# A hybrid decoder layer on one Trainium2 core: index scores in pieces of at most 512 columns placed between input-projection products, the sample tile alternating with tile 7, and the sample's index steps between chunks of u and q

## What is computed

```python
h = rms_norm(x, ln1)
u, q, k, v, qi, ki, wi, gates = split(h @ w_in)
# index scores: for every query and causal key, over 4 index heads
score[t, s] = sum_h w[t, h] * relu(qi[t, h] . ki[s])
idx = top_k(score, 256)                  # ties: lower position first
out = softmax_attention(q, k[idx], v[idx], bias)
pool = causal windows 2/4/8/16 over u, minus u, then a linear map
x = x + merge(pool, out, sigmoid(gates)) @ w_out ; then the FFN
```

## Time and profile before

| what | us |
|---|---|
| median of 3 runs | 1776.0 (1774.52 to 1786.52) |
| profiled execution, device time | 1784.01 |
| its span, first to last instruction | 1782.2 |
| PE busy in the span | 1672.0 (94%) |
| DVE / ACT / POOL busy | 775.4 / 478.9 / 447.4 |

### The profile page before, as it was taken

One profiled execution on the slowest core, in us unless ns is written; L12 is line 12 of the kernel. 1 busy time (PEld: TensorE's weight loads), 2 busy tenths in 40 slices (PEclk: granted clock), 3 DMA queues, 4 the chain that ended last, 5 costly groups with the idle time before them and its releaser, 6 DMA issues.

```text
span 1782.2 us, 25675 instructions
## 1 busy us (share of the span) xinstructions
PE 1672.0 (94%) x10060; PEld 1425.0 (80%) x10060; DVE 775.4 (44%) x1927; ACT 478.9 (27%) x923; POOL 447.4 (25%) x379
## 2 busy tenths in 40 slices
PE   7997799688999998899999999999999999999997
PEld 4544366445569866688889999999999999999996
DVE  2215999997910066511244442323323323323315
ACT  2113211154452255521143322111121121111113
POOL 3000107220524432111112252232232232232220
PEclk9996899899999999999999999999999999999999
DMA  5500511072651000122301231111111111111002
GB/s 174 105 21 24 172 36 37 12 272 88 195 189 48 24 1 1 44 78 82 95 25 36 71 95 48 41 46 43 36 50 44 47 47 47 47 47 47 0 1 107
DMA packets 115842, 116.95 MB, mean 66 GB/s; under 512 B 17438, under 2 KB 104110, under 8 KB 112685
## 3 DMA queue, kind: packets, MB, share of 16 engines
q1 hardware_dynamic: 102471, 73.74, 13.8%
q0 software_dynamic: 5312, 39.33, 6.9%
q10 hardware_dynamic: 7982, 2.83, 0.6%
HBM read 107.66 MB, written 8.45 MB: 65 GB/s over the span
## 4 chain that ended last, share of the span: by engine, by line
PE 55%; DVE 1%; ACT 1%; DMA 0%; issue 0%; DVEq 0%; ACTq 0%
PE banks L108 52%; PE banks L1669 3%; DMA out_dram<-yo 0%; DVE yo L1993 0%; PE banks L1658 0%; ACT XH L1826 0%; DVE rinv L1958 0%; ACT junk L1900 0%; ACT sH L1819 0%; ACT resid L1823 0%; PE banks L1761 0%; PE banks L1707 0%; DVE gated L1913 0%; ACT fst L1902 0%; ACT rinv L1870 0%
## 5 line engine op out<-in xcount | busy, mean ns | idle before, releaser
L108 PE MATMUL banks<-hnH,wH 128*128 128x344 f32 x1056 | 338.7, 321 | 3.8 <-DVE sg L1967 3.8
L108 PE MATMUL banks<-hnH,wL 128*128 128x344 f32 x1056 | 337.4, 320 | 0.0
L1791 POOL TENSOR_TENSOR wL<-w_raw,wH 128x1024 fp32r<-128x1024 f32 (+1 forms) x55 | 155.8, 2849 | 204.2 <-ACT wH L1850 203.8
L108 PEld LDWEIGHTS banks<-hnH,wH 128*128 128x128 f32 x1056 | 198.9, 188 | 4.4 <-issue 4.3
L108 PEld LDWEIGHTS banks<-hnH,wL 128*128 128x128 f32 x1056 | 198.8, 188 | 0.0
L1981 DVE TENSOR_TENSOR resid<-resid,banks 128x344 f32<-128x344 f32 x264 | 134.9, 512 | 107.4 <-PE banks L108 107.3
L1339 DVE TENSOR_SCALAR_CACHE_REDUCE pta<-SC,thr 128x384 uint8<-128x384 f32 (+2 forms) x192 | 176.1, 942 | 4.6 <-POOL SC L835 2.5
L108 PE MATMUL banks<-aH,wH 128*128 128x344 f32 x528 | 169.4, 321 | 1.6 <-DVE resid L1981 1.6
L108 PE MATMUL banks<-aH,wL 128*128 128x344 f32 x528 | 169.7, 321 | 0.0
L108 PE MATMUL banks<-hnL_lo,wH 128*128 128x344 f32 x528 | 169.0, 320 | 0.0
L108 PE MATMUL banks<-aL,wH 128*128 128x344 f32 x528 | 168.5, 319 | 0.0
(11 more groups left out here) (295 smaller groups left out, 2924.7 us busy)
## 6 DMA issues: line engine op xcount, KB each, us to landing
w_raw<-in_w_gate_up_dram SPq DMA_DIRECT2D x44, 512.0 KB, 3.9
w_raw<-in_w_down_dram SPq DMA_DIRECT2D x11, 1024.0 KB, 4.8
big<-in_w_in_dram SPq DMA_DIRECT2D x12, 512.0 KB, 4.0
W<-in_x_prompt_dram SPq DMA_DIRECT2D x8, 512.0 KB, 6.9
slab_raw<-in_w_in_dram SPq DMA_DIRECT2D x8, 512.0 KB, 4.3
x_nat<-in_x_prompt_dram SPq DMA_DIRECT2D x8, 512.0 KB, 4.1
slab_raw<-in_w_out_dram SPq DMA_DIRECT2D x8, 512.0 KB, 4.0
out_dram<-yo SPq DMA_DIRECT2D x8, 512.0 KB, 2.6
```

The costliest lines, as they stand in the source:

```text
L108: last = nc.tensor.matmul(out, w_cols(w, k), x_cols(x, k), start=(k == 0 and j == 0), stop=(k == nk - 1 and j == 2))
L1791: gp.tensor_tensor(wL[p], w_raw[p], f32(wH[p]), ALU.subtract).then_inc(w_lo, 1)
```

## The change

It does these things:

1. The scores are cut into 40 units of at most 512 columns, on banks 2 and 3. The units of tile i stand between the products of natural tile i + 3 (tiles 2 to 4) and between the products of u chunks 0, 1, 2 (tiles 5, 6, 7). Relu and sums go by unit.
2. Natural tiles 7 and 8 are made together, their products alternating.
3. Natural transposes go to banks 0 and 1, two tiles late, in the middle of a natural.
4. u and q chunks use three banks (5 to 7); chunk 3 stands in the sample index's set-up, chunks 4 to 10 between the requests' transposes and products, 11 to 13 between the last steps, 14 to 23 behind. The loops are written out.
5. The tie sums go from in front of the cached-key steps to behind step 12 (`TIES_AT`).
6. On DVE the masks of tiles 4 and 5 go behind the sample's mask, and the sample's softmax steps from inside the last bisection to in front of it; the PE steps beside the pool projections move by one.
7. `kid`, `kidT`, relu's buffers and the scratch of x's squares lie elsewhere, so the first two gathers of index keys no longer wait for the scores.

The diff, cut to its core:

```diff
+            TIES_AT = 12
+            UNITS = [(i, h, c0, min(512, lens[i] - c0)) for i in range(FIRST_TOPK, NBLK) for h in range(IH) for c0 in range(0, lens[i], 512)]
...
+                def score_unit(n):
+                    i, h, c0, w = UNITS[n]
+                    half = slice(h % 2 * HD, h % 2 * HD + HD)
+                    pe.wait_ge(natT_evac, i + 1)
+                    if n >= 2:
+                        pe.wait_ge(relu_done, n - 1)
+                    mm(ps[:, 2 + n % 2, 0:w], qiT[half, h // 2, tile_cols(i)], kiT[half, c0:c0 + w], start=True, stop=True).then_inc(idx_ready, 1)
...
+                def natural(tiles, scored):
+                    for t in tiles:
...
+                        pe.wait_ge(hT_ready, 2 * t + 2)
+                        if t >= 2:
+                            pe.wait_ge(nat_evac, t - 1)
+                    for q in range(2 * KD):
+                        k = q % KD
+                        for t in tiles:
...
+                        if scored and q % (2 * KD // len(scored)) == 0:
+                            score_unit(scored[q * len(scored) // (2 * KD)])
+                        if q == KD - 1 and tiles[0] >= 2:
+                            transpose_natural(tiles[0] - 2)
...
+                def slab_chunk(x, scored=()):
...
+                    if x < NCH:
+                        pe.wait_ge(nat_evac, NT)
+                    else:
+                        pe.wait_ge(uq_evac, x - 2)
+                    for k in range(KD):
+                        last = mm(ps[:, 5 + x % 3, 0:CH], big[:, n % 2, k, :], hT[:, k, chunk(c)], start=k == 0, stop=k == KD - 1)
+                        if scored:
+                            score_unit(scored[k])
...
+                slab_chunk(0, units_of(5))
+                transpose_natural(NT - 2)
+                slab_chunk(1, units_of(6))
                 transpose_natural(NT - 1)
+                slab_chunk(2, units_of(7))
...
+                slab_chunk(3)
                 pe.wait_ge(zi_copied, 1)
...
+                    if b < NB - 1:
+                        slab_chunk(4 + b)
                     pe.wait_ge(kidT_evac, b + 1)
...
+                slab_chunk(11)
                 pe.wait_ge(sidx_relu, 1)
...
+                slab_chunk(12)
                 pe.wait_ge(ssp_done, 1)
...
+                    if m == TIES_AT:
+                        sum_sample_ties()
...
-                        if blocks == (6, 7) and r == 20:
-                            sample_max()
-                            sample_negmax()
-                            sample_weights()
...
-                for k, i in enumerate((2, 3, 4, 5)):
+                for k, i in enumerate((2, 3)):
...
+                for k, i in ((2, 4), (3, 5)):
+                    to_mask(k, i)
+                sample_max()
+                sample_negmax()
+                sample_weights()
                 bisect_pair(slice(5, 7), (6, 7), 5 * BITS, 4 * BITS + 2)
```

More of the change, by code:

```diff
@@ L480, in _ @@
                 transpose_x(0)
[L481 to L486, removed]
+                for t in range(NT - 1):
+                    if t >= 3:
+                        pe.wait_ge(natT_evac, t - 2)
+                    transpose_x(t + 1)
+                    if t < NT - 2:
+                        natural((t,), units_of(t - 3))
+                    else:
+                        natural((t, t + 1), units_of(t - 3))
@@ new lines, in _, with sum_sample_ties @@
+                last.then_inc(stT_ready, 1)
+                slab_chunk(13)
+                pe.wait_ge(uq_evac, 12)
+                for g in range(NG):
+                    last = tr(ps[0:POOLBUF + NB, 1, g * P:(g + 1) * P], U[:, g, 16 + SEQ - POOLBUF:16 + TOK], ident[:, :])
+                last.then_inc(uT_ready, 1)
+                for x in range(14, UQ):
+                    slab_chunk(x)
+                def sum_sample_ties():
+                    pe.wait_ge(sm_step, SM["ties"])
+                    pe.wait_ge(upto_made, 1)
+                    mm(ps[:, 6, 0:P + 2], same16[:, :, :].rearrange("p b r -> p (b r)"), seq[:, :], start=True, stop=True)
+                    mm(ps[:, 6, 256:256 + P + 1], upto16[:, :], seq[:, 0:P + 1], start=True, stop=True).then_inc(sm_made, 1)
@@ new lines, in _ @@
+                pool.wait_ge(setup_step, 8)
+                load_kid(0)
+                load_kid(1)
+                for i in range(FIRST_TOPK, NBLK - 2):
+                    causal(i)
+                pool.wait_ge(nat_evac, NT)
+                for f in range(2):
+                    gp.tensor_tensor(zw[:, f * 32:(f + 1) * 32].rearrange("b (c h) -> b c h", c=NB),
+                                     ident[0:NB, 0:NB].unsqueeze(2).to_broadcast([NB, NB, IH]),
+                                     wiN[0:NB, NBLK, :].unsqueeze(1).to_broadcast([NB, NB, IH]), ALU.mult).then_inc(zw_made, 1)
@@ L843, in _ @@
+                causal(NBLK - 2)
+                causal(NBLK - 1)
+                for b in range(2, NB):
+                    pool.wait_ge(kid_used, b - 1)
+                    load_kid(b)
                 pool.wait_ge(setup_step, 3)
@@ L863, in did @@
                     ins.then_inc(mix_step, 1)
-                pool.wait_ge(uq_evac, 6 + 12)
+                pool.wait_ge(uq_evac, 12)
                 pool.wait_ge(stT_evac, 1)
-                pool.wait_ge(sidx_used, NB)
+                pool.wait_ge(ssc_ready, 1)
+                for b in range(2):
+                    pool.wait_ge(nat_out[b], 48 * len(range(b, NT, 2)))
                 did(gp.tensor_copy(sx[:, :, :, POOLBUF], U[:, :, 16 + SEQ:16 + TOK]))
@@ L1025, in _ @@
                   ACT.Copy).then_inc(qid_ready, 1)
+                for x in range(3):
+                    for n in units_of(5 + x):
+                        relu_unit(n)
+                    uq_out(x)
                 act.wait_ge(zi_ready, 2)
```

235 lines of the change are left out of this document (102 added, 133 removed).

## The result

Measured beside each other, the changed kernel takes 1829.2 us (median) and the kernel before 1781.3 us; the ratio is 1.0252, 95% interval 1.0214 to 1.0291. The forecast was 1788 with a range of 1770 to 1808: the direction of its likeliest case was right, the size was not. On the profiled executions, of which the sum was made, the spans are 1782.2 and 1827.5 us: **+45 instead of +12**.

A forecast was written before the change was run, and what follows sets the result against it. PE bound the kernel, with DVE's selection 26 us behind; delayed 37.5 us, DVE would take over. Gates 11.7 us later plus 0.3 made +12 on the 1776 us median, or 1788, range 1770 to 1808.

The forecast's parts named there:

- likeliest case: DVE's last mask comes late and sets the gates: 11.7 us later, span +12, time 1788 us; chance 0.73.
- slack: How much later DVE's selection may end before it delays the first gate product: 26 us.
- the remainder of the chain: DVE's work from the sample scores being ready, at 266, to its last mask, at 528.2.
- The request at 7.74 us: Sample index on PE: each request takes 3.10 us plus a 4.64 us chunk that hides the wait for ACT's copy.
- PE up to the sample scores: PE's new order summed as far as `ss_ready`, which the second bisection awaits: 266 us, bounds 243 and 281.
- naturals as before, "128.4": PE's naturals end as now at 129.0, less one group of five transposes: 128.4 us.
- a possible drop of the clock: At u chunk 0 on PE, behind a 3.2 us wait, the clock may drop, costing 0.7 us.
- changes into and out of a unit: PE's stationary-shape changes around the 40 score units: 80 at 0.12 us, 9.6 us in all.
- chunk 12 behind the small products: Last u chunk before `ss_ready` on PE, behind L530 and L532, priced like other chunks at 4.64 us.
- rival 2: Clock stays low through scores and chunks 0 to 2: `ss_ready` 32 us later, time 1820; chance 0.10.
- the 45 us of idle PE before the gates: PE, 33 us ahead, reaches the end of the pool projections and waits some 45 us for DVE's mask through ACT.
- plus 0.3: Behind the gate start, PE's restart at half clock costs about what it does today, plus 0.3 us.

The follow-up runs named there:

- a_ht_first: Changed kernel with DVE copying tile t+1's transposed x before scaling tile t+2; ratio 1.0227, span 1815.4 us.
- e_kv_early: Changed kernel with ACT copying tile 7's key and value bank in mid-naturals, u chunk 0 waiting for that copy alone; ratio 1.0196, span 1814.0 us.
- f_serial: Changed kernel with the naturals of tiles 7 and 8 one after the other instead of alternating; ratio 1.0173, span 1810.1 us.
- i_three_causes: Changed kernel with DVE's transposed-x copy first, tile 7's key/value bank copied early, and naturals 7 and 8 in series; ratio 1.0102, span 1796.6 us.
- b_ss_early: Changed kernel with u chunks 4 to 12 moved behind the transpose of SP1, so the sample-index steps stand together; ratio 1.0202, span 1818.5 us.

## Why the prediction was wrong

**Right, and shown.** That DVE's chain takes over and sets the gates; its slack (26, measured 25.7); PE's wait before the ties behind step 12 (17 to 20, came 18.9); the remainder of the chain (528.2 - 266 = 262.2 us forecast, 264.4 measured); the 3.5 us from the last mask to the gates (3.65). The request at 7.74 us, with ACT's copy and the gathers hidden, came at 7.66. The alternation was forecast at 3.0 us and cost 2.8. DVE's wait before the second bisection was forecast at 20 us and came at 20.4, but by luck in part: the end of the first bisection (forecast 246, came 274.5) and `ss_ready` were late by nearly the same.

**Wrong: the term "PE up to the sample scores", 266 instead of 294.9.** Term by term:

| term of the sum | forecast, us | measured, us |
|---|---|---|
| naturals as before, "128.4" | no new wait | +12.2 (a_ht_first) |
| the wait before chunk 0 and "a possible drop of the clock" behind it | 3.2 + 0.7 | 13.2 (e_kv_early), some 11 of it clock |
| changes into and out of a unit | 0.12 each, 9.6 | 0.39 a unit, 15.6 |
| alternation with the 8-row tile | 3.0 | 2.8 (f_serial) |
| chunk 12 behind the small products | 4.6 | 6.4 |

The excesses are 12.2 + 9.3 + 6.0 - 0.2 + 1.8 = 29.1, and the total is 28.9. The 12.2 hold the 1.0 us that was there ahead of the edit, so the sum closes to about 1 us and no better.

The first line is a step that failed, not a size: the working listed the waits that the change adds at tiles 7 and 8 and at chunk 0, and passed over the new `hT_ready` in `transpose_natural`, because before the change x's preparation was never late by more than 1.4 us in PE's rows. On ACT it stood behind 9 us of output issues, hidden. Of what was measured, 3.4 us are the lower clock behind the two stalls, for which the sum had no term at all.

The second was named as rival 2, with chance 0.10 and 32 us, for a clock low through three chunks. It stayed low through one, 11 us of loss: what the rival described, a clock brought down by this wait, happened at a third of its size. Whether the 64-row products kept it down is not shown. The term of 0.7 us assumed that the clock comes back almost at once behind the wait. In the forecast's own rows the clock stood at 0.50 over 21 us with PE busy for 19.5 of them, which spoke against that.

The third had its price from two places where the shape changes for one product. Around a unit both changes count. A chunk step with its 384-column unit takes 192.16 - 190.54 = 1.62 us, of which 0.58 is the product of the chunk (4.64 / 8) and 0.645 the unit (384 at 1.68 ns); with a 512-column one 204.72 - 202.89 = 1.83, less 0.58 and 0.86: 0.39 each time.

```profile
190.54 0.85 PE L531 MATMUL banks<-hT,big 128*128 128x344 f32 x2
191.32 0.91 PE L471 MATMUL banks<-I 64*128 64x384 f32 x2
192.16 0.84 PE L531 MATMUL banks<-hT,big 128*128 128x344 f32 x2
...
202.89 0.84 PE L531 MATMUL banks<-hT,big 128*128 128x344 f32 x2
203.66 1.12 PE L471 MATMUL banks<-I 64*128 64x512 f32 x2
204.72 0.85 PE L531 MATMUL banks<-hT,big 128*128 128x344 f32 x2
```

TensorEngine Tiling (Array Packing), section Key Properties, in the Trainium skill, says that changing the tiling mode drains TensorE; the 0.39 us agree with a drain in kind, and the page gives no figure.

The last line, chunk 12: in its 6.4 us the granted clock was 0.50 from about 289 to 292.3 (some 1.7 us of loss), with no stall of PE in front of it since one of 1.11 us at 277.5.

```profile
287.51 6.59 PE L531 MATMUL banks<-hT,big 128*128 128x344 f32 x16
```

**Wrong beside that, without effect on the time:** the 45 us of idle PE before the gates. The working set PE's 33 us of gain against DVE's delay as if the wait at the ties were gone, and in the same forecast had 17 to 20 us of wait there. The two waits share what PE is ahead: 18.9 + 34.5 = 53.4 us in the changed kernel, 16.3 + 34.7 = 51.0 in i_three_causes.

**Wrong and small: "plus 0.3" behind the gate start.** It came at +2.3. The clock was at 0.50 for 2.4 us longer than before, which accounts for 1.2 us; b_ss_early has as little of it as the kernel before and still +2.1, so the rest stays open.

That the three corrections together land on 265.3 is in part luck: that kernel has no alternation and no pause at chunk 0, which the forecast's 266 included with 6.9 us, and has 7.8 us of dearer unit changes and chunk 12 in their place. What the agreement does show is the chain behind it.

**The range.** With the slack used up, each us of error in `ss_ready` is a us of the result, so the range should have been at least as wide as the bounds of that sum, and its upper bound of 281 priced the changes of shape double but held no unknown wait and no longer stretch of low clock.

## What to carry to other kernels

Before making a busy engine busier, find the other long chain and what it needs first: here 19 us of gate start were to be had by moving the tie sums and the softmax steps alone, and every us that delayed DVE's input beyond its slack was lost. When a wait is added in the middle of a stage, look up how late the awaited producer really is in the trace of before, on its own engine and on the one behind it, and not at how long the consumer waited. An idle engine in front of a late input can be filled with rounds of work whose inputs are complete.

## What the runs showed of the hardware

- A pause of 2.24 us (1.90 in a second kernel) behind 60 us or more at full clock was followed by the lower clock level for some 24 us (20), though PE was busy without a gap behind it, with 64-row products between the others; a pause of 1.34 us, or of 0.32 us, in the same place was not. Stalls of 6.64 and 2.38 us with only 128-row products behind them were followed by some 3.3 us of it each.
- One 64-row product between 128-row float32 products cost 0.39 us beside its columns, at 384 and at 512 columns alike; alternating the products of a 128-token and an 8-token tile cost 2.8 us over 32 products.
- Two of ACT's DMA issues for one tile's outputs took 4.30 and 4.53 us, one for the next tile 3.96, and the others of these tiles 0.34 to 0.58; ACT did nothing else meanwhile.
